# A three-block transformer step on one core: GpSimd takes three of eight low halves in five norms, and linear attention sums its two key sets on VectorE before the diagonal product

## The chip, the core and the metric

The kernel runs on one core of a Trainium2 chip. The metric is the device time of one execution in microseconds (us); lower is better. Engines: PE is TensorE, DVE is VectorE, ACT is ScalarE, POOL is GpSimd, SP is the queue that issues weight loads.

## What is computed

Input x is 512 tokens by 1024 features in float32. Two blocks of a first model and one of a second follow each other:

```python
for i in range(2):                        # first model
    h = modulate(rms_norm(x, g), shift, scale)
    y = nsa_mixer(h) if i == 0 else swa_sink_mixer(h)
    x = x + (1 + g1) * rms_norm(y, g)
    h = modulate(rms_norm(x, g), shift2, scale2)
    x = x + (1 + g2) * rms_norm(squared_relu_mlp(h), g)
h = rmsnorm(x, norm_mix)                  # second model
# linear attention, neighbourhood attention, cross attention on h, gated and summed,
# then x = x + (...) @ w_out and a convolutional FFN on rmsnorm(x, norm_ffn)
```

The linear attention has 8 heads of width 128 and is summed over both directions of time:

```python
f = lb + (1 - lb) * sigmoid(zf);  k = (1 - lb) * sigmoid(-zf)   # one zf for each direction
scores[t, s] = sum_k q[t, k] * k[s, k] * prod(f between s and t)
o = (scores @ v)_forward + (scores @ v)_backward
```

At t = s no decay stands between the two, so the diagonal of the scores is q·k for each direction, and the output needs the sum of both.

## The kernel before

All activations are kept transposed, features on the 128 partitions and 512 tokens along the free dimension, so a matrix of 1024 features is 8 chunks of 128x512. Every weight product keeps float32 precision with fp32r matmuls: a number is split into a rounded high half and a low half, and a product is high·high + high·low + low·high, three matmuls a chunk, 24 for a panel of 128 output features. The panels follow each other for the whole kernel; they alternate between two PSUM banks `PA` and two halves of the weight buffers. SP loads a panel into `RAW`; POOL makes its high half (L658) and then its low half (L665); both are 128x1024 reads and writes of SBUF. POOL starts on a panel when PE has finished the high products of the panel two before it (semaphore `w_hi_used`), and SP loads the next one when POOL has made the low half.

The list `RUNS` (L270 to L348) is the written order of panels. The queues of SP, POOL and PE all walk it with `walk` (L350): a run of equal panels becomes a hardware loop, and an entry that is a string makes POOL do other work at that place. "residual" is such an entry: POOL adds three of the eight residual chunks (`add_pooled`, L673) between the weight panels.

**A norm** (`norm`, L1818, `round_hi`, L1318, `first_pair`, L791). When the inverse root of the mean square is in PSUM, three engines work chunk by chunk: DVE multiplies chunk k into a PSUM bank `PO` (L1826), ACT writes its rounded high half to `H[0]` (L1327 with a shift, L1325 without), DVE writes the low half, full minus high, to `H[1]` (L1835 or L1833). PE follows in `first_pair` with two panels at once: per chunk two matmuls with the high half (L802), one with the low half of the weight (L804), then a wait for `h_lo` and two matmuls with the low half of the activation (L807). After chunk 7 there are eight more matmuls of the second panel (L813). There are seven such norms: memory tokens, the first norm of x, and five later ones, at about 522, 905, 1120, 1492 and 2319 us.

**Linear attention** (PE L1175 to L1214, ACT L1596, DVE L2228 to L2288). For each head PE goes through ten levels (`lv`), each followed by half of a weight panel of the next head (`panel_half`, 12 matmuls), which keeps PE in work while DVE and ACT prepare the next level. Level 0 is the diagonal: for each of four 128-token blocks a product of the forward keys `R[:, KF]` with q and one of the backward keys `R[:, KB]` with q, summed in PSUM (L1192, L1193). These are plain float32, and each appears in the trace as two matmuls. Levels 1 to 7 use keys that ACT copies to `HK` (L1602), and levels 8 and 9 the larger blocks. `prepare(h)` (L2228) stands on DVE between head h-1 and head h: the floor of the forget gates (L2233, whose semaphore `level_qk` releases level 0 on PE), a copy of it (L2235), and two products with q (L2236, L2237), the second of which releases ACT's keys of level 1.

Of the kernel before, what the change touches and what calls it, by code (L numbers as in the profile page):

```python
# [19 lines left out]
F32 = mybir.dt.float32  # L20
# [83 lines left out]
def build(nc, T, out):  # L104
# [237 lines left out]
    OUT0["mix"] = count_panels()  # L342
    run(8, DC, lambda i: panel(w_out2, 0, DC, i * P))
    for g in range(2):
        run(GC, DC, lambda i, g=g: panel(w_up2, 0, DC, (g * GC + i) * P),
            lambda i, g=g: panel(w_up2, 0, DC, (FFC + g * GC + i) * P))
        OUT0["ffn"] = count_panels()
        run(8, GC, lambda i, g=g: panel(w_dn2, g * GC, GC, i * P))  # L348

# [61 lines left out]
        return T["ada_w"][l, (m % DC) * P:(m % DC + 1) * P, g * ADA_N:(g + 1) * ADA_N]  # L411

    POOLED = [1, 3, 5]
    DVE_OWN = [k for k in range(DC) if k not in POOLED]
    RESIDUAL_ORDER = [1, 0, 3, 2, 5, 4, 6, 7]
    NORM_MIX, MEM_NORM, NORM_FFN, NORM_FINAL, GNORM, COND = 64, 72, 80, 88, 96, 97
# [232 lines left out]
    @block.gpsimd  # L649
    def _(pool):  # L650
        pool.memset(zeros[:], 0.0).then_inc(sem("zeros_set"), 1)
        pool.wait_ge(sem("zeros_set"), 1)

        def split_hi(e, p, s, kc):
            if not isinstance(p, int) or p >= 2:
                e.wait_ge(w_hi_used, p - 1)
            e.wait_ge(w_loaded[s], ((p - s) * 16) + 32 if not isinstance(p, int) else (p // 2 + 1) * 32)
            e.tensor_tensor(W[0][:, s, 0:kc], RAW[:, s, 0:kc], zeros[:, 0:1].rearrange("p (a b) -> p a b", b=1).broadcast_to([P, kc, P]),  # L658
                            ALU.add).then_inc(w_hi, 1)

        def split_lo(e, p, s, kc):
            e.wait_ge(w_hi, p + 1)
            if not isinstance(p, int) or p >= 2:
                e.wait_ge(panel_ready, p - 1)
            e.tensor_tensor(W[1][:, s, 0:kc], RAW[:, s, 0:kc], W[0][:, s, 0:kc].bitcast(F32), ALU.subtract).then_inc(w_split, 1)  # L665

        def split(e, p, s, kc, loads):
            split_hi(e, p, s, kc)
            split_lo(e, p, s, kc)

        c = Counts()

        def add_pooled():  # L673

            for k in POOLED:
                c["weighed"] += 1
                pool.wait_ge(sem("weighed_y"), c["weighed"])
                pool.tensor_tensor(X[:, k, :], X[:, k, :], Y[:, k, :], ALU.add).then_inc(sem("x_pooled"), 1)

        def scale_weights(which, fills):  # L680

            if which == "residual":
                add_pooled()
                return
            plan = PLANS[which]
            for i, (G, b) in enumerate(plan.units):
                grp, u = plan.groups[G], c["unit"] + i
                nk, v = grp["keys"][b], u % 8
                inverse = stat[3][:, v:v + 1]
                pool.wait_ge(sem("inverted"), u + 1)  # L690
                at = int(grp["sink"] is not None)
                w = plan.weights[i % len(plan.weights)][:, at:at + nk]
                if grp["all"]:
                    pool.tensor_tensor(blocks4(w), blocks4(w), each4(inverse4, grp), ALU.mult).then_inc(sem("scaled"), 1)
                elif grp["gate"] is None:
                    pool.tensor_scalar(w, w, inverse, None, ALU.mult).then_inc(sem("scaled"), 1)  # L696
# [12 lines left out]

    @block.tensor  # L710
    def _(pe):
# [79 lines left out]
        def first_pair(x, n):  # L791

            p, ready = c["panel"], c["normed"] - DC
            a, b = p % 2, 1 - p % 2
            if p >= 2:
                pe.wait_ge(panel_free, p)
            pe.wait_ge(w_split, p + 2)
            for k in range(DC):
                hi, lo, last = x[0][:, k, 0:n], x[1][:, k, 0:n], k == DC - 1
                pe.wait_ge(sem("h_hi"), ready + k + 1)  # L800
                for s in (a, b):
                    pe.matmul(PA[s][:, 0:n], W[0][:, s, k], hi, start=(k == 0), stop=False)  # L802
                if not last:
                    pe.matmul(PA[a][:, 0:n], W[1][:, a, k], hi, start=False, stop=False)  # L804
                pe.wait_ge(sem("h_lo"), ready + k + 1)
                for s in (a, b):
# [369 lines left out]
        for h in range(8):  # L1176
            R, q = HR[h % 2], HQ[h % 2]
            for lv in range(10):
                r = c["level"]
                if 1 <= lv <= 7:  # L1180
                    pe.wait_ge(sem("level_k"), 7 * h + lv)
                else:
                    pe.wait_ge(sem("level_qk"), r + 1)
                if r >= 2:
                    pe.wait_ge(sem("level_taken"), r - 1)
                if lv == 9:
# [2 lines left out]
                for b in range(NT):  # L1189
                    cols_b = slice(b * P, b * P + P)  # L1190
                    if lv == 0:
                        pe.matmul(bank[:, cols_b], R[:, KF, cols_b], q[:, cols_b], start=True, stop=False)  # L1192
                        mm = pe.matmul(bank[:, cols_b], R[:, KB, cols_b], q[:, cols_b], start=False, stop=True)  # L1193
                    elif lv <= 7:
                        mm = pe.matmul(bank[:, cols_b], HK[:, lv % 2, cols_b], two_sides(R, QB, QF, b * P, P, LEVELS[lv - 1]), start=True, stop=True)
                    elif lv == 8:
# [65 lines left out]
    def _(act):  # L1262
# [52 lines left out]
        def root(N=S, bank=PS[0]):  # L1315
            act.activation(roots[:, 0:N // P], bank[:, 0:N // P], ACT.Sqrt, bias=sl("eps"), scale=1.0 / D).then_inc(sem("rooted"), 1)

        def round_hi(dst, n, shift, N=S, at=0):  # L1318

            for k in range(n):  # L1320
                r = c["normed"]
# [2 lines left out]
                if shift is None:  # L1324
                    act.activation(hi, full, ACT.Copy).then_inc(sem("h_hi"), 1)  # L1325
                else:
                    act.activation(hi, full, ACT.Identity, bias=shift(k), scale=1.0).then_inc(sem("h_hi"), 1)  # L1327
                c["normed"] += 1

        def rotary_hi(p, turned):  # L1330
# [94 lines left out]
                    for m in range(DC * (3 + g) + 2, min(DC * (4 + g) + 2, 6 * DC)):  # L1425
                        mod_load(m)

        def apply(shift, dst=H, N=S):
            round_hi(dst, DC, shift, N)
            act.wait_ge(sem("h_lo"), c["normed"])  # L1430

        def norm(shift):
            squares(xs, DC, added=True)
            c["x_ready"] += len(DVE_OWN)
            c["x_pooled"] += len(POOLED)
            inverse_root()
            apply(shift)

        xs = lambda k: X[:, k, :]
        ys = lambda k: Y[:, k, :]  # L1440
# [61 lines left out]
        mem_value_copy(3)  # L1502
        phi_load(1)
        round_hi(H, DC - 3, lambda k: mod(0, 0)(k + 3), at=3)
        act.wait_ge(sem("h_lo"), c["normed"])
        act.wait_ge(sem("angle"), 1)
        act.activation(sinT[:], sinT[:], ACT.Sin)
        act.activation(cosT[:], cosT[:], ACT.Sin, bias=sl("half_pi"), scale=-1.0).then_inc(sem("tables"), 1)
# [186 lines left out]
                open_gate(k + 2)  # L1695
        act.dma_start(X[:], x_spill).then_inc(sem("x_back"), 16)
        panel_squares(xs, OUT0["mix"])
        apply(None)
        for g in range(2):
            for k in range(GC):  # L1700
                act.wait_ge(sem("conv_a"), g * GC + k + 1)
# [18 lines left out]
    def _(dve):  # L1720
# [94 lines left out]
            dve.tensor_tensor(tmp[3][:, 0:N].rearrange("p (b n) -> p b n", b=nb), ident.rearrange("p (b n) -> p b n", b=1).broadcast_to([P, nb, P]),  # L1815
                              roots[:, 4:4 + nb].rearrange("p (b n) -> p b n", n=1).broadcast_to([P, nb, P]), ALU.mult).then_inc(sem("diagonal"), 1)

        def norm(src, scale, shift, dst=H, N=S, inverse=PS[1]):  # L1818

            for i in range(DC + 1):  # L1820
                if i < DC:
                    r = c["normed"]
                    if r >= 2:
                        dve.wait_ge(sem("h_lo"), r - 1)
                        dve.wait_ge(sem("h_hi"), r - 1)
                    dve.scalar_tensor_tensor(PO[r % 2][:, 0:N], src(i), scale(i), inverse[:, 0:N], ALU.mult, ALU.mult).then_inc(sem("normed"), 1)  # L1826
                    c["normed"] += 1
                if i >= 1:
                    r, k = c["h_lo"], i - 1
                    full, hi, lo = PO[r % 2][:, 0:N], dst[0][:, k, 0:N].bitcast(F32), dst[1][:, k, 0:N]  # L1830
                    dve.wait_ge(sem("h_hi"), r + 1)
                    if shift is None:
# [1 line left out]
                    else:  # L1834
                        dve.scalar_tensor_tensor(lo, full, shift(k), hi, ALU.add, ALU.subtract).then_inc(sem("h_lo"), 1)  # L1835
                    c["h_lo"] += 1

        def inverse_here():

# [256 lines left out]
            taken(lambda bank: dve.tensor_copy(cols[:, r, 0:c_rows[r]], bank[:, 0:c_rows[r]]))  # L2096
        dve.wait_ge(sem("turned_taken"), c["turned"])
        dve.wait_ge(sem("inverse"), 1)
        norm(ym, col1(MEM_NORM), None, MH, 256)
        dve.wait_ge(sem("cond_sig"), 1)  # L2100
        link(dve.tensor_tensor(small[:, 0:8], cols[:, 1, COND:COND + 8], small[:, 8:16], ALU.mult))
        mod_step(0)
# [11 lines left out]

        dve.wait_ge(sem("inverse"), 2)
        dve.wait_ge(sem("turned_taken"), 20)
        norm(xs, coef(0, 0), mod(0, 0), inverse=PT[0])
        dve.wait_ge(sem("tables"), 1)

        def add_positions(side, k):  # L2120
# [107 lines left out]
        def prepare(h):  # L2228
# [2 lines left out]
            dve.wait_ge(panel_free, HG0 + 5 * h + 4)  # L2231
            dve.wait_ge(sem("turned_taken"), c["turned"])
            dve.tensor_scalar(HTP[:], HT[h % 2][:], 1e-12, None, ALU.max).then_inc(sem("level_qk"), 1)  # L2233
            dve.wait_ge(sem("level_qk"), 10 * h + 1)
            dve.tensor_copy(HT[h % 2][:], HTP[:]).then_inc(sem("hg_floor"), 1)  # L2235
            dve.tensor_tensor(R[:, QF, :], HTP[:, 0, :], q[:], ALU.mult)  # L2236
# [163 lines left out]
```

## Time and profile before

| | us |
|---|---|
| median of 3 runs | 2705.49 |
| the three runs | 2708.56, 2705.10, 2705.49 |
| the profiled execution | 2709.62 |
| its span, from first to last instruction | 2707.8 |
| PE busy | 2529.4 |
| POOL busy | 1772.6 |
| DVE busy | 1347.7 |
| ACT busy | 711.8 |

The profiled execution is one run, 4.1 us above the median, and 1.8 us of it lie outside the span. A busy share of PE near 100% does not mean full speed: the ends of matmuls are modelled, so the distance between starts is what counts, and a granted clock of 1.00 stands for 2.4 GHz and 0.50 for 1.2 GHz.

### The profile page before, as it was taken

Reading aid. Unit: us, or ns where it says so; the run is one execution under the profiler, and the core shown is the slowest. Engines: PE = TensorE matmul, PEld = TensorE weight load, DVE = VectorE, ACT = ScalarE, POOL = GpSimd, SP = SyncE. Lnnn points to the kernel's source line nnn. Section 1 sums busy time; section 2 is a strip of 40 time slices with the busy share of each in tenths; the row PEclk is TensorE's granted clock in tenths of the full one; section 3 lists DMA queues with packets and bytes.
Section 4 is the critical chain, followed back from the end, with each engine's and each line's share of the span. In section 5 each row is a group of like instructions: output and inputs, shape, how many; then the busy total and the mean of one; then the engine's idle time right before and its main releaser. Section 6 shows DMA issues by size and latency. Waiting matters only on the chain. (4 is left out here: it accounts for less than half of the span.)

```text
span 2707.8 us, 36598 instructions
## 1 busy us (share of the span) xinstructions
PE 2529.4 (93%) x11854; PEld 2049.4 (76%) x11854; DVE 1347.7 (50%) x2632; ACT 711.8 (26%) x1498; POOL 1772.6 (65%) x983
## 2 busy tenths in 40 slices
PE   7898889899999888899999999999999889999998
PEld 6686667688888667688886777777878776787877
DVE  6367887443442566412213567674128434752552
ACT  4204776211101245301112223232017232100001
POOL 5364445587777576577776545455769767787884
PEclk9898989999999889899999999999999999999999
DMA  8383000254653212233332221212323213233332
GB/s 292 117 240 97 1 1 24 89 184 150 205 186 89 59 40 75 69 101 93 99 95 85 86 63 58 60 57 69 100 85 77 74 55 117 85 96 91 93 105 74
DMA packets 420545, 259.73 MB, mean 96 GB/s; under 512 B 62844, under 2 KB 411513, under 8 KB 414017
## 3 DMA queue, kind: packets, MB, share of 16 engines
q1 hardware_dynamic: 390896, 195.28, 25.0%
q10 hardware_dynamic: 29521, 62.82, 7.1%
q8 instruction: 71, 1.16, 0.2%
q14 instruction: 57, 0.47, 0.1%
HBM read 253.86 MB, written 8.10 MB: 97 GB/s over the span
## 5 line engine op out<-in xcount | busy, mean ns | idle before, releaser
L658 POOL TENSOR_TENSOR W<-RAW,zeros 128x1024 fp32r<-128x1024 f32 (+2 forms) x355 | 678.1, 1910 | 687.7 <-PE PA L741 328.7
L665 POOL TENSOR_TENSOR W<-RAW,W 128x1024 fp32r<-128x1024 f32 (+2 forms) x355 | 850.5, 2396 | 31.7 <-PE PA L749 5.1
L738 PE MATMUL PA<-H,W 128*128 128x512 f32 x1272 | 500.8, 394 | 6.0 <-POOL W L658 2.1
L741 PE MATMUL PA<-H,W 128*128 128x512 f32 x1272 | 498.3, 392 | 0.0
L738 PE MATMUL PA<-A,W 128*128 128x512 f32 x944 | 374.8, 397 | 16.2 <-DVE A L1973 10.8
L741 PE MATMUL PA<-A,W 128*128 128x512 f32 x944 | 372.2, 394 | 0.0
L749 PE MATMUL PA<-H,W 128*128 128x512 f32 x1272 | 314.3, 389 | 0.0
L738 PEld LDWEIGHTS PA<-H,W 128*128 128x128 f32 x1272 | 240.2, 189 | 59.7 <-POOL W L658 6.5
L741 PEld LDWEIGHTS PA<-H,W 128*128 128x128 f32 x1272 | 240.2, 189 | 50.4 <-issue 0.5
L749 PEld LDWEIGHTS PA<-H,W 128*128 128x128 f32 x1272 | 238.7, 188 | 49.5
L749 PE MATMUL PA<-A,W 128*128 128x512 f32 x944 | 238.6, 395 | 0.0
L738 PEld LDWEIGHTS PA<-A,W 128*128 128x128 f32 x944 | 178.8, 189 | 59.4 <-issue 14.0
L749 PEld LDWEIGHTS PA<-A,W 128*128 128x128 f32 x944 | 180.4, 191 | 38.2
L741 PEld LDWEIGHTS PA<-A,W 128*128 128x128 f32 x944 | 178.9, 190 | 35.4
L1421 ACT ACTIVATE tmp<-PA 128x512 f32<-128x512 f32 x64 | 38.3, 598 | 520.2 <-PE PA L749 514.7
L696 POOL TENSOR_SCALAR pr<-pr,stat_inv 128x256 f32<-128x256 f32 (+2 forms) x112 | 136.6, 1229 | 49.0 <-DVE stat_inv L1932 48.4
L698 POOL TENSOR_SCALAR pr<-pr,stat_inv,gate 128x128 f32<-128x128 f32 (+3 forms) x128 | 88.2, 689 | 117.0 <-DVE stat_inv L1932 116.9
L2043 DVE SCALAR_TENSOR_TENSOR PA<-PA,tmp 128x512 f32<-128x512 f32 x64 | 44.8, 700 | 235.7 <-ACT tmp L1421 235.7
L1367 ACT ACTIVATE pr<-sc,stat_neg 128x128 f32<-128x128 f32 (+3 forms) x240 | 133.8, 557 | 103.4 <-DVE stat_neg L1920 101.2
L779 PE MATMUL PA<-H,W 128*128 128x512 f32 x320 | 133.4, 417 | 0.0
L780 PE MATMUL PA<-H,W 128*128 128x512 f32 x320 | 125.1, 391 | 0.0
L1702 ACT ACTIVATE tmp<-tmp 128x512 f32<-128x512 f32 x22 | 13.9, 633 | 276.5 <-DVEq L2348 276.5
(367 smaller groups left out, 3974.8 us busy)
## 6 DMA issues: line engine op xcount, KB each, us to landing
AD<-in_ada_w_dram ACTq DMA_DIRECT2D x40, 1024.0 KB, 5.1
RAW<-in_w_in_dram SPq DMA_DIRECT2D x160, 256.0 KB, 3.2
RAW<-in_mlp_w_up_dram SPq DMA_DIRECT2D x128, 256.0 KB, 3.1
RAW<-in_mlp_w_down_dram SPq DMA_DIRECT2D x128, 256.0 KB, 3.1
RAW<-in_w_up_dram SPq DMA_DIRECT2D x88, 256.0 KB, 3.1
RAW<-in_nsa_w_in_dram SPq DMA_DIRECT2D x40, 256.0 KB, 4.2
RAW<-in_w_down_dram SPq DMA_DIRECT2D x16, 384.0 KB, 3.4
RAW<-in_swa_w_in_dram SPq DMA_DIRECT2D x20, 256.0 KB, 3.3
```

The lines of the kernel that those rows point to most:

```text
L658: e.tensor_tensor(W[0][:, s, 0:kc], RAW[:, s, 0:kc], zeros[:, 0:1].rearrange("p (a b) -> p a b", b=1).broadcast_to([P, kc, P]), ALU.add).t ...
L665: e.tensor_tensor(W[1][:, s, 0:kc], RAW[:, s, 0:kc], W[0][:, s, 0:kc].bitcast(F32), ALU.subtract).then_inc(w_split, 1)
L696: pool.tensor_scalar(w, w, inverse, None, ALU.mult).then_inc(sem("scaled"), 1)
L698: pool.tensor_scalar(w, w, inverse, grp["gate"][b], ALU.mult, ALU.mult).then_inc(sem("scaled"), 1)
L738: pe.matmul(PA[s][:, 0:n], W[0][:, s, k], hi, start=(k == 0), stop=False)
L741: mm = pe.matmul(PA[s][:, 0:n], W[0][:, s, k], lo, start=False, stop=False)
L749: mm = pe.matmul(PA[s][:, 0:n], W[1][:, s, k], x[0][:, k, 0:n], start=False, stop=(k == kc - 1))
L779: pe.matmul(PA[s][:, :], W[0][:, s, k], H[0][:, k, :], start=(k == 0), stop=False)
L780: mm = pe.matmul(PA[s][:, :], W[0][:, s, k], H[1][:, k, :], start=False, stop=False)
L1367: act.activation(plan.weights[i % ring][:, 0:nk], sc[u % 2][:, 0:nk], ACT.Exp, bias=neg, scale=-1.0, accum_out=stat[2][:, v:v + 1]).then_i ...
L1421: act.activation(tmp[q][:], PA[s][:], ACT.Relu).then_inc(sem("mlp_relu"), 1)
L2043: dve.scalar_tensor_tensor(PA[s][:], PA[s][:], 0.0, tmp[q][:], ALU.max, ALU.mult).then_inc(sem("mlp_square"), 1)
```

## The change

Two edits that do not touch each other.

Norms: in the five later norms the low halves of chunks 1, 3 and 5 are made by POOL. Since POOL works from SBUF here, ACT writes for these chunks, beside the high half, a full copy to `tmp[4]` or `tmp[5]`; POOL subtracts, and PE waits for the new semaphore `h_low` in place of `h_lo`. The first run of the last norm's panels is split into 2 and 20 panels, so that POOL's three subtractions have a place between them.

Linear attention: DVE adds both key sets of a head into `HK[:, 0]`, right after the floor that releases level 0 on PE; PE waits for that sum and makes one product per block.

```diff
-        run(GC, DC, lambda i, g=g: panel(w_up2, 0, DC, (g * GC + i) * P),
-            lambda i, g=g: panel(w_up2, 0, DC, (FFC + g * GC + i) * P))
+        if g == 0:
+            run(1, DC, lambda i: panel(w_up2, 0, DC, 0), lambda i: panel(w_up2, 0, DC, FFC * P))
+            RUNS.append("norm")
+        a = 1 if g == 0 else 0
+        run(GC - a, DC, lambda i, g=g, a=a: panel(w_up2, 0, DC, (g * GC + i + a) * P),
+            lambda i, g=g, a=a: panel(w_up2, 0, DC, (FFC + g * GC + i + a) * P))
...
+    LOW_POOLED = [1, 3, 5]
...
+        def subtract_pooled():
+            for j, k in enumerate(LOW_POOLED):
+                n = c["h_full"]
+                pool.wait_ge(sem("h_full"), n + 1)
+                pool.tensor_tensor(H[1][:, k, :], tmp[4 + j % 2][:], H[0][:, k, :].bitcast(F32), ALU.subtract).then_inc(sem("h_low"), 1)
+                c["h_full"] += 1
...
             if which == "residual":
                 add_pooled()
+            if which in ("residual", "norm"):
+                subtract_pooled()
                 return
...
-                pe.wait_ge(sem("h_lo"), ready + k + 1)
+                name = "h_low" if k in pooled else "h_lo"
+                c[name] += 1
+                pe.wait_ge(sem(name), c[name])
...
+                if lv == 0:
+                    pe.wait_ge(sem("keys_added"), h + 1)
...
-                        pe.matmul(bank[:, cols_b], R[:, KF, cols_b], q[:, cols_b], start=True, stop=False)
-                        mm = pe.matmul(bank[:, cols_b], R[:, KB, cols_b], q[:, cols_b], start=False, stop=True)
+                        mm = pe.matmul(bank[:, cols_b], HK[:, 0, cols_b], q[:, cols_b], start=True, stop=True)
...
+                if k in pooled:
+                    j = pooled.index(k)
+                    if j >= 2:
+                        act.wait_ge(sem("h_low"), c["h_full"] - 1)
+                    whole = tmp[4 + j % 2][:]
+                    if shift is None:
+                        act.activation(whole, full, ACT.Copy).then_inc(sem("h_full"), 1)
+                    else:
+                        act.activation(whole, full, ACT.Identity, bias=shift(k), scale=1.0).then_inc(sem("h_full"), 1)
...
-                    if r >= 2:
-                        dve.wait_ge(sem("h_lo"), r - 1)
+                    if i >= 2:
                         dve.wait_ge(sem("h_hi"), r - 1)
+                        if i - 2 in pooled:
+                            dve.wait_ge(sem("h_full"), c["h_full"] + pooled.index(i - 2) + 1)
+                        else:
+                            dve.wait_ge(sem("h_lo"), c["h_lo"])
...
-                if i >= 1:
+                if i >= 1 and i - 1 not in pooled:
...
             dve.tensor_scalar(HTP[:], HT[h % 2][:], 1e-12, None, ALU.max).then_inc(sem("level_qk"), 1)
+            dve.tensor_tensor(HK[:, 0, :], R[:, KF, :], R[:, KB, :], ALU.add).then_inc(sem("keys_added"), 1)
             dve.wait_ge(sem("level_qk"), 10 * h + 1)
             dve.tensor_copy(HT[h % 2][:], HTP[:]).then_inc(sem("hg_floor"), 1)
             dve.tensor_tensor(R[:, QF, :], HTP[:, 0, :], q[:], ALU.mult)
```

## Rows read from the trace of the kernel before

**Rows 1.** The page, part 1: busy time of each engine, share, instructions

```profile
PE 2529.4 (93%) x11854; PEld 2049.4 (76%) x11854; DVE 1347.7 (50%) x2632; ACT 711.8 (26%) x1498; POOL 1772.6 (65%) x983
```

**Rows 2.** Timeline of the norm at 522 us: PE, then DVE, then ACT (start, us, engine)

```profile
523.73 1.19 PE L802 MATMUL PA<-H,W 128*128 128x512 f32 x2 [3.07 <-ACT H L1327]
531.65 0.72 PE L807 MATMUL PA<-H,W 128*128 128x512 f32 x2
534.80 1.98 PE L813 MATMUL PA<-H,W 128*128 128x512 f32 x8
...
522.11 1.42 DVE L1826 SCALAR_TENSOR_TENSOR PO<-X,coefA,PS 128x512 f32<-128x512 f32 x2 [5.78 <-ACT PS L1313]
...
522.90 1.35 ACT L1327 ACTIVATE H<-PO,modT 128x512 fp32r<-128x512 f32 x2 [0.88 <-DVE PO L1826]
```

**Rows 3.** Source L807: for whom its weight loads waited (us, times)

```profile
  DVE H L1835: 0.8, 2
```

**Rows 4.** Timeline of PE in the norm at 1120 us, second chunk

```profile
1123.81 1.05 PE L802 MATMUL PA<-H,W 128*128 128x512 f32 x2
```

**Rows 5.** Sources L678 and L1852: ns min/median/max of each form, first and last start

```profile
L678 POOL TENSOR_TENSOR X<-X,Y x12: 1265/1268/1273, 508.1 to 1482.4; 128x512 f32<-128x512 f32 x12
...
L1852 DVE SCALAR_TENSOR_TENSOR X<-PT,coefA,X x20: 751/751/752, 508.7 to 1485.7; 128x512 f32<-128x512 f32 x20
```

**Rows 6.** Timeline at the start of head 1: PE, DVE, POOL

```profile
1567.80 0.49 PE L1192 MATMUL PS<-sinT,Y 128*128 128x128 f32 x2
1569.61 0.48 PE L779 MATMUL PA<-H,W 128*128 128x512 f32 x1
...
1566.52 1.23 DVE L2233 TENSOR_SCALAR HTP<-hg_T 128x1024 f32<-128x1024 f32 x1
1577.46 0.69 DVE L2268 TENSOR_TENSOR Y<-Y,HTP 128x512 f32<-128x512 f32 x1 [6.06 <-PE PS L1195]
...
1567.09 1.89 POOL L658 TENSOR_TENSOR W<-RAW,zeros 128x1024 fp32r<-128x1024 f32 x1 [3.80 <-PE PA L780]
```

**Rows 7.** Timeline at the start of head 2: DVE and POOL

```profile
1611.65 1.23 DVE L2233 TENSOR_SCALAR HTP<-hg_T 128x1024 f32<-128x1024 f32 x1
...
1612.13 1.90 POOL L658 TENSOR_TENSOR W<-RAW,zeros 128x1024 fp32r<-128x1024 f32 x1 [3.61 <-PE PA L780]
```

**Rows 8.** Timeline at the start of head 0: PE, DVE, POOL

```profile
1527.03 0.79 PE L1192 MATMUL PS<-cosT,Y 128*128 128x128 f32 x2 [2.65 <-DVE HTP L2233]
1530.30 0.48 PE L779 MATMUL PA<-H,W 128*128 128x512 f32 x1
...
1525.75 1.22 DVE L2233 TENSOR_SCALAR HTP<-hg_T 128x1024 f32<-128x1024 f32 x1
...
1524.66 2.35 POOL L665 TENSOR_TENSOR W<-RAW,W 128x1024 fp32r<-128x1024 f32 x1
```

**Rows 9.** Timeline of the FFN: DVE and POOL

```profile
2336.87 1.51 DVE L2351 TENSOR_TENSOR tmp<-tmp 128x512 f32<-128x512 f32 x1
...
2335.94 1.89 POOL L658 TENSOR_TENSOR W<-RAW,zeros 128x1024 fp32r<-128x1024 f32 x1
```

**Rows 10.** Busy time by stretches: PE busy, ..., granted clock third from the end

```profile
2147.97:2151.97 4.00, 4.00 (x18) 3.31 (x19) 0.00 (x0) 0.00 (x0) 3.92 (x3) 1.00 0.44 131
2280.85:2284.85 4.00, 4.00 (x11) 3.13 (x12) 0.59 (x1) 0.00 (x0) 3.97 (x2) 0.57 0.03 8
1056.80:1060.80 4.00, 3.98 (x14) 2.07 (x14) 4.00 (x7) 3.98 (x7) 0.00 (x0) 1.00 0.92 281
1528.00:1890.00 362.00, 355.08 (x1789) 288.88 (x1788) 234.94 (x415) 95.03 (x139) 175.40 (x82) 1.00 0.21 60
```

**Rows 11.** Timeline of PE: the gaps that end where three of those stretches begin

```profile
1056.82 0.47 PE L738 MATMUL PA<-A,W 128*128 128x512 f32 x1 [2.38 <-DVE A L1973]
2147.97 0.50 PE L738 MATMUL PA<-H,W 128*128 128x512 f32 x1 [1.56 <-ACTq L1267]
2280.85 0.64 PE L738 MATMUL PA<-H,W 128*128 128x512 f32 x1 [2.07 <-POOL W L658]
```

More of the change, by code:

```diff
@@ L793, in first_pair @@
             p, ready = c["panel"], c["normed"] - DC
+            pooled = LOW_POOLED if p >= 16 else []
             a, b = p % 2, 1 - p % 2
@@ L1316, in root, with round_hi @@
             act.activation(roots[:, 0:N // P], bank[:, 0:N // P], ACT.Sqrt, bias=sl("eps"), scale=1.0 / D).then_inc(sem("rooted"), 1)
-        def round_hi(dst, n, shift, N=S, at=0):
+        def round_hi(dst, n, shift, N=S, at=0, pooled=()):
             for k in range(n):
@@ L1327, in round_hi @@
                     act.activation(hi, full, ACT.Identity, bias=shift(k), scale=1.0).then_inc(sem("h_hi"), 1)
+                if k in pooled:
[7 more added lines that the diff above has]
+                        act.activation(whole, full, ACT.Identity, bias=shift(k), scale=1.0).then_inc(sem("h_full"), 1)
+                    c["h_full"] += 1
+                else:
+                    c["h_lo"] += 1
                 c["normed"] += 1
@@ L1426, in mlp, with apply @@
                         mod_load(m)
-        def apply(shift, dst=H, N=S):
-            round_hi(dst, DC, shift, N)
-            act.wait_ge(sem("h_lo"), c["normed"])
+        def apply(shift, dst=H, N=S, pooled=()):
+            round_hi(dst, DC, shift, N, pooled=pooled)
+            act.wait_ge(sem("h_lo"), c["h_lo"])
+            act.wait_ge(sem("h_low"), c["h_full"])
         def norm(shift):
@@ L1436, in norm @@
             inverse_root()
-            apply(shift)
+            apply(shift, pooled=LOW_POOLED)
         xs = lambda k: X[:, k, :]
@@ L1504, in _ @@
         round_hi(H, DC - 3, lambda k: mod(0, 0)(k + 3), at=3)
-        act.wait_ge(sem("h_lo"), c["normed"])
+        act.wait_ge(sem("h_lo"), c["h_lo"])
         act.wait_ge(sem("angle"), 1)
@@ L1697, in _ @@
         panel_squares(xs, OUT0["mix"])
-        apply(None)
+        apply(None, pooled=LOW_POOLED)
         for g in range(2):
@@ L1816, in rstd, with norm @@
                               roots[:, 4:4 + nb].rearrange("p (b n) -> p b n", n=1).broadcast_to([P, nb, P]), ALU.mult).then_inc(sem("diagonal"), 1)
-        def norm(src, scale, shift, dst=H, N=S, inverse=PS[1]):
+        def norm(src, scale, shift, dst=H, N=S, inverse=PS[1], pooled=LOW_POOLED):
             for i in range(DC + 1):
@@ L1822, in norm @@
                     r = c["normed"]
-                    if r >= 2:
-                        dve.wait_ge(sem("h_lo"), r - 1)
+                    if i >= 2:
                         dve.wait_ge(sem("h_hi"), r - 1)
+                        if i - 2 in pooled:
+                            dve.wait_ge(sem("h_full"), c["h_full"] + pooled.index(i - 2) + 1)
+                        else:
+                            dve.wait_ge(sem("h_lo"), c["h_lo"])
                     dve.scalar_tensor_tensor(PO[r % 2][:, 0:N], src(i), scale(i), inverse[:, 0:N], ALU.mult, ALU.mult).then_inc(sem("normed"), 1)
                     c["normed"] += 1
-                if i >= 1:
-                    r, k = c["h_lo"], i - 1
+                if i >= 1 and i - 1 not in pooled:
+                    k, r = i - 1, c["normed"] - (1 if i == DC else 2)
                     full, hi, lo = PO[r % 2][:, 0:N], dst[0][:, k, 0:N].bitcast(F32), dst[1][:, k, 0:N]
@@ L1836, in norm @@
                     c["h_lo"] += 1
+            c["h_full"] += len(pooled)
+            if pooled:
+                dve.wait_ge(sem("h_full"), c["h_full"])
         def inverse_here():
@@ L2098, in _ @@
         dve.wait_ge(sem("inverse"), 1)
-        norm(ym, col1(MEM_NORM), None, MH, 256)
+        norm(ym, col1(MEM_NORM), None, MH, 256, pooled=[])
         dve.wait_ge(sem("cond_sig"), 1)
@@ L2116, in _ @@
         dve.wait_ge(sem("turned_taken"), 20)
-        norm(xs, coef(0, 0), mod(0, 0), inverse=PT[0])
+        norm(xs, coef(0, 0), mod(0, 0), inverse=PT[0], pooled=[])
         dve.wait_ge(sem("tables"), 1)
```

## Prediction

> **What bounds the kernel now.** I first read the page for the engine that is busy throughout: PE, 2529.4 us or 93% of the span [rows 1]. DVE and POOL have time left on average, so the question is where PE waits for them or is made to. Then I read the timelines of the two stages that the diff touches. In a norm PE starts 1.6 us after DVE and then follows chunk by chunk; in linear attention it stands still only at the head of each head, for the floor of the forget gates. There the granted clock is 1.00 over the whole stage [rows 10]. What counts is when PE starts and what it waits for; busy time on DVE counts only through that. Last I looked for what a new DVE instruction with both inputs in SBUF does beside POOL, since the change puts one in front of PE eight times, and for what PE's clock does after short gaps.
>
> **Norms, five times.** Per norm the change takes 3 low halves from DVE, adds 3 full copies on ACT and gives POOL 3 subtractions. DVE's pace with both operations is one chunk in about 1.45 us. PE's is 5 matmuls a chunk. Their starts are 0.227 us apart at clock 1.00 (eight of them span 1.98 us, the last one's modelled length being 0.39) and 0.43 at half clock [rows 2, 4]: 1.1 and 2.1 us a chunk. PE starts the norm after a gap and is at half clock for its first two or three chunks, so it falls behind DVE and needs almost the rest of the norm to catch up. All that the weight loads of the low products waited for DVE is 0.8 us, twice, over the whole kernel [rows 3]; both fall in the norm at 522 us. With the pitches around them, that norm would end 0.5 us earlier if DVE were never late. The other four gain nothing.
>
> Is POOL in time? In the norm at 522 us DVE's first two products end at 523.5, ACT's two high halves at 524.25 [rows 2]; the full copy costs another 0.69 (524.95), and POOL's subtraction 1.27, taken from its addition of the same size [rows 5]: 526.3. By the same walk the low half of chunk 3 is ready at 528.6 and that of chunk 5 at 530.9. PE reads the latter at 531.65 [rows 2], and, counting back two chunks of 1.13 us at a time, chunk 3 near 529.3 and chunk 1 near 527.0. POOL has nothing else to do there: its next weight panel waits until the last low product of the norm. So POOL's work is hidden, with margins of 0.6 us; without that cover each late low half would cost up to 0.5. ACT's 3 copies fit between its high halves, which now take half of its time. DVE's wait for the full copies ends where the next product would start anyway. The run of FFN panels that is split in two changes no load: the first two panels were split on POOL before that norm as well. Term: **-0.5 us**; bounds -3 (PE begins several norms at clock 1.00, and DVE's pace would then have cost it) and +1.5.
>
> **Linear attention, what PE saves.** Level 0 now runs from 1567.80 to 1569.61, 1.81 us for 16 matmuls, 0.113 each [rows 6]. Half of them go: 0.90 us a head. In head 0, where the clock is at half, it is 3.27 us for 16 [rows 8], so 1.64 go. The Trainium skill (TensorE: Matmul & The Clock Gate, "Wait — 56ns, not 53.3ns?") gives 55.6 ns from start to start for 128 columns at full clock. That would make the saving half as large, 0.45 a head, and the sum 3.2 us worse; the trace does not agree for these float32 products, and it decides.
>
> **What PE waits for instead.** The addition stands behind the floor on DVE and in front of the copy and both products with q. Alone it would cost what the nearest DVE operation does, some 0.55 to 0.7 us. But it is not alone. In head 1 the floor ends at 1567.75, while POOL makes a high half from 1567.09 to 1568.98 [rows 6]; in head 2 the floor ends at 1612.88 and POOL's high half at 1614.03 [rows 7]. The other five heads repeat these two patterns, four in all with 1.23 us left of the high half and three with 1.15. This is geometry, not chance: POOL is released by PE's own half panel, and DVE by PE's level 9 just before it.
>
> What a DVE operation with two SBUF inputs does then is seen in the FFN: L2351 starts at 2336.87, while POOL's high half runs until 2337.83, and ends at 2338.38 after 1.51 us instead of 0.69 [rows 9]. It does nothing until POOL's instruction ends, then needs 0.55. It gets its turn before POOL's next instruction, which follows 0.08 us later. The Trainium skill (SBUF — State Buffer, "Who interferes with whom") has it as a rule: a VectorE instruction with two SBUF inputs and a GpSimd instruction that reads SBUF lock each other out; the trace agrees, with that row.
>
> So the addition ends 1.23 + 0.55 = 1.78 or 1.15 + 0.55 = 1.70 us after the floor, 1.74 on average, and PE's level 0 starts that much later. Net per head: 1.74 - 0.90 = +0.84; for seven heads **+5.9 us**. In head 0 POOL ends at 1527.01, just as the floor does [rows 8]: the addition costs 0.6, the saving is 1.64, and about two later matmuls move into the half clock (0.4): **-0.6 us**.
>
> Nothing takes this back or adds to it later in the head. The copy, the products with q, the gate and the taking of level 0 all come 1.7 us later on DVE, but DVE then idles 6.06 us for PE's level 1 [rows 6]; ACT's keys of level 1 come 1.7 us later too, but PE first has half a panel and the values of the last head to work off, and DVE sees level 1 done only at 1577.46 [rows 6], 7.9 us after level 0 has begun. POOL's low half starts up to 0.5 us later and is wanted only two levels on.
>
> **The clock.** PE will stand still some 1.75 us before level 0 in seven heads, where the half panel runs into level 0 without a gap that the timeline shows today [rows 6]. After a gap of 1.56 us in dense work the clock stayed at 1.00, after one of 2.07 it was 0.57 over the next 4 us, after one of 2.38 it stayed at 1.00 [rows 10, 11]. So a gap of this size can cost the clock, and sometimes does. One such drop costs 4.0 x (1 - 0.57) = 1.7 us. The bounds are no head (0) and all seven (+11.9). I take three heads, nearer to the middle than to either end, as 1.75 lies between a gap that kept the clock and a shorter gap than 2.38 that lost it: **+5.1 us**.
>
> **Sum.** -0.5 - 0.6 + 5.9 + 5.1 = +9.9 us. For the profiled execution that is 2709.62 + 9.9 = 2719.5; it stands 4.1 above the median of the runs, so the median becomes 2705.49 + 9.9 = **2715.4 us**. A measurement of this kernel can tell 0.2%, 5.4 us, from no change: 2700.1 to 2710.9 is "same".
>
> **Rivals.**
> *The clock holds.* The gap never costs the clock; all else as above: +4.8, 2710.3, inside "same". For it: the 1.56 us gap, and full clock in the whole stage today. Against it: 2.07 us lost it, and level 0 behind the gap is thin work. Chance 0.22.
> *The addition is not held up.* It runs beside POOL's high half, or gets in before it. Then a head costs 0.6 - 0.9 = -0.3, seven -2.1, and with head 0 and the norms -3.2: 2702.3, not slower. The place is the start of heads 1 to 7; the point from which it decides is a delay of the addition behind POOL of 0.3 us: below it the head gains, above it it loses. For it: DVE passes POOL freely when one of its inputs is in PSUM, and a shift of the floor by 0.6 us to the front would be enough. Against it: the row in the FFN, with the same POOL instruction. Chance 0.12.
> *The norms give more.* Without the low halves DVE is never the pace, and in norms where PE begins at clock 1.00 up to 1.3 us each are won. With the addition not held up as well this reaches -7: 2698. The trace shows PE behind, not DVE. Chance 0.04.
> *Held by both halves.* DVE doesn't get in between POOL's two instructions (0.08 us apart) and waits for the low half too, 2.4 us more a head, +17 on top: 2727 with the clock held. Against it: it did get in at 2337.83. Chance 0.07.
> *The forecast*, with one to seven heads at half clock: 2712 to 2722, chance 0.55.
>
> The range for 8 in 10 takes in the forecast, the held clock and the free addition: 2702.0 to 2722.5. Faster by over 0.2%: 0.04. Same: 0.22 + 0.12 = 0.34. Slower: 0.55 + 0.07 = 0.62.
>
> **What would show it.** In the timeline of heads 1 to 7 the addition should be 1.7 to 1.8 us long and end 0.55 us after POOL's high half; PE's gap before level 0 should be near 1.75 us with DVE's `hg_K` as its releaser, and level 0 should last 0.9 us. An addition of 0.7 us beside a running POOL instruction would prove the main step wrong. The granted clock of the stage, 1.00 today, should fall below 1: each head that lost it takes about 0.5% off the stage's mean. In the norms PE's last eight matmuls should start at the same distance from DVE's first product as now, 0.5 us less at 522 us; a wait of PE for POOL's low half of over 0.5 us would prove the hidden part wrong. The prediction fails as a whole if the distance from one level 0 to the next shrinks.

## The result, and the profile after the change

| us | before | after |
|---|---|---|
| median of 6 runs | 2705.4 (2704.55 to 2709.32) | 2716.5 (2711.14 to 2718.91) |
| ratio, 95% interval | | 1.0037 (1.0027 to 1.0047) |
| profiled execution | 2709.62 | 2716.51 |
| its span | 2707.8 | 2714.4 |
| mean granted clock | 0.967 | 0.965 |

The kernel became slower by 0.37%. The same kernel measured once more, beside the kernel before and its own parts (`e6_after_again`), gave 1.0025 (1.0015 to 1.0036). The forecast was 2715.4 us. (Ratios here are made from all runs of both kernels, so they can differ a little from the quotient of the medians.) The two profiled executions are only 6.9 us apart, since the one of before stands 4.1 above the median of its first runs; so the views below explain some 6.6 us of span, and not 11.

The page of the kernel after, part 1:

```profile
PE 2523.2 (93%) x11790; PEld 2046.2 (75%) x11790; DVE 1348.1 (50%) x2625; ACT 719.3 (26%) x1513; POOL 1793.6 (66%) x998
```

PE is busy for 6.2 us less than in [rows 1] and the program is longer: the busy totals say nothing of this change, only the waits do. Now the timeline at the start of head 1 of the linear attention, as in [rows 6]. Line numbers have moved: the floor is L2271, the addition L2272, level 0 on PE L1212.

```profile
1566.77 1.23 DVE L2271 TENSOR_SCALAR HTP<-hg_T 128x1024 f32<-128x1024 f32 x1
...
1567.34 1.89 POOL L663 TENSOR_TENSOR W<-RAW,zeros 128x1024 fp32r<-128x1024 f32 x1 [3.80 <-PE PA L795]
1567.91 1.87 DVE L2272 TENSOR_TENSOR hg_K<-Y 128x512 f32<-128x512 f32 x1
...
1569.31 2.72 POOL L670 TENSOR_TENSOR W<-RAW,W 128x1024 fp32r<-128x1024 f32 x1
1569.70 1.21 DVE L2274 COPY hg_T<-HTP 128x1024 f32<-128x1024 f32 x1
...
1569.88 1.13 PE L1212 MATMUL PS<-sinT,hg_K 128*128 128x128 f32 x8 [1.80 <-issue]
1570.76 0.48 PE L794 MATMUL PA<-H,W 128*128 128x512 f32 x1
```

The floor ends at 1568.00. The addition ends at 1569.78, which is 1.78 us later and 0.55 after POOL's high half (1567.34 + 1.89 = 1569.23). PE follows at 1569.88, after 1.80 us of standing still. Level 0 then has 8 matmuls and takes 0.88 us, from 1569.88 to the next panel's first matmul at 1570.76, where [rows 6] had 16 in 1.81 by the same measure. The addition over all eight heads, from the source view of its line:

```profile
L2272 DVE TENSOR_TENSOR hg_K<-Y x8: 690/1826/1870, 1526.0 to 1844.1; 128x512 f32<-128x512 f32 x8
```

690 ns is head 0: there the addition starts at 1525.95, POOL's low half ends at 1526.10, and no other POOL instruction follows for 10 us. The seven others are held up. The starts of level 0 in heads 2 and 3 show the same twice over, with the two patterns of the forecast:

```profile
1615.86 1.13 PE L1212 MATMUL PS<-cosT,hg_K 128*128 128x128 f32 x8 [1.72 <-issue]
...
1661.93 1.13 PE L1212 MATMUL PS<-sinT,hg_K 128*128 128x128 f32 x8 [1.80 <-issue]
```

From one head to the next it takes 46.0 us, against 45.16 before. The waits of PE in this stage:

```profile
PE PS L1212 <- issue: 12.4, 7, 1.8
PE PS L1212 <- DVE hg_K L2272: 3.3, 1, 3.3
```

12.4 us in seven waits, 1.77 each, and the profile writes them down to "issue". Only in head 0 does it name `hg_K`. A blocked DVE instruction counts as busy from its issue on, so no idle time stands anywhere that would lead to POOL; the cause shows only where the rows of DVE and POOL are laid side by side.

The clock, in stretches of 8 us around three of the seven gaps and over the whole stage (columns as in [rows 10]):

```profile
1566.00:1574.00 8.00, 6.20 (x31) 4.83 (x30) 7.26 (x9) 1.48 (x2) 4.61 (x2) 1.00 0.18 52
1612.00:1620.00 8.00, 6.28 (x31) 4.89 (x30) 7.25 (x9) 1.48 (x2) 4.60 (x2) 1.00 0.19 55
1658.00:1666.00 8.00, 6.20 (x31) 4.88 (x30) 7.32 (x9) 1.48 (x2) 4.60 (x2) 1.00 0.16 48
...
1528.00:1895.00 367.00, 347.74 (x1720) 282.00 (x1720) 246.03 (x421) 94.72 (x139) 176.09 (x82) 0.99 0.20 58
```

The granted clock stays at 1.00 after the gap, here and in the four other heads. The 0.99 of the stage comes from head 0 alone, in the stretches at its start:

```profile
1526.80:1530.20 3.40, 3.40 (x12) 3.11 (x13) 2.86 (x4) 0.86 (x1) 0.00 (x0) 0.50 0.55 154
1530.20:1533.60 3.40, 3.40 (x11) 2.65 (x11) 0.00 (x0) 0.00 (x0) 0.00 (x0) 0.60 0.00 0
1533.60:1537.00 3.40, 3.40 (x19) 2.99 (x18) 2.02 (x4) 0.70 (x1) 0.16 (x1) 1.00 0.00 0
```

In the trace of before the second of these stretches is at 1.00 already.

### The profile page after: what moved, and what is told of

Same layout as the page of the kernel before. It is cut to its first block and busy times, and to the rows that moved or that the text cites. A ratio compares the mean times of both kernels' runs of the same rounds, so it can differ in the third digit from the quotient of the medians.

```text
span 2714.4 us, 36469 instructions
## 1 busy us (share of the span) xinstructions
PE 2523.2 (93%) x11790; PEld 2046.2 (75%) x11790; DVE 1348.1 (50%) x2625; ACT 719.3 (26%) x1513; POOL 1793.6 (66%) x998
```

## The experiments

Ten kernels ran, in three groups on three chips, each timed against the kernel before beside it. They start from the kernel after; `...` marks lines left out of an edit. "Keys only" means: the list `LOW_POOLED` is empty, so that the norms are those of before, and linear attention is as after.

**The two halves by themselves.** `e1_norms_only` takes the addition and its wait out and puts the two products back; `e2_keys_only` empties the list, and with it goes ACT's wait for POOL's low halves.

```diff
-    LOW_POOLED = [1, 3, 5]
+    LOW_POOLED = []
...
-            act.wait_ge(sem("h_low"), c["h_full"])
```

> The norms' half of the change alone, against the kernel before. Main theory (PE is behind DVE in four of the five norms, POOL's low halves come in time): -0.5 us, between -3 and +1.5, and from DVE's first product to PE's last eight matmuls the same times as before within 0.3 us wherever the clock falls alike. Rival (DVE's low halves were the pace): -1 to -1.3 us a norm, -5 to -6 in all. Rival (POOL is late, PE waits for it): more than +0.5 us a norm.

Measured: 2709.2 us against 2708.81, ratio 0.9997 (0.9988 to 1.0006). The norms' half makes no difference that can be told, and the rival of -5 to -6 us is excluded. Its trace missed one point: the norm at 908 us, with PE at full clock throughout, took 11.7 us, where such norms take 12.6 to 13.1 without this half; 0.3 had been allowed.

> The linear attention's half alone, no low half on POOL. Main theory (the sum of the keys stands behind POOL's high half): the addition lasts 1.78 to 1.87 us in heads 1 to 7 and 0.69 in head 0, each head from 1 on is 0.84 us longer, the stage +6 to +7.5 us, and the whole kernel +6 to +11 us. Rival (the loss of the whole change comes from the norms or from a clock that falls there): within 3 us of the kernel before.

Measured: 2714.47 against 2708.81, ratio 1.0024 (1.0014 to 1.0034), 46.0 us a head, clock 1.00 over the stage. By the medians that is +5.7 us, just below the +6 expected, and by the ratio +6.5. All of the slowdown that can be told is in linear attention, and the two ratios multiplied, 1.0021, agree with the 1.0025 of the second measurement of the whole change.

**Who starts first.** `e3_add_first` is the whole change with the two DVE instructions in the other order. PE's level 0 waits for `keys_added` alone.

```diff
-                if 1 <= lv <= 7:
+                if lv == 0:
+                    pe.wait_ge(sem("keys_added"), h + 1)
+                elif lv <= 7:
                     pe.wait_ge(sem("level_k"), 7 * h + lv)
...
-                if lv == 0:
-                    pe.wait_ge(sem("keys_added"), h + 1)
...
+            dve.tensor_tensor(HK[:, 0, :], R[:, KF, :], R[:, KB, :], ALU.add).then_inc(sem("keys_added"), 1)
             dve.tensor_scalar(HTP[:], HT[h % 2][:], 1e-12, None, ALU.max).then_inc(sem("level_qk"), 1)
-            dve.tensor_tensor(HK[:, 0, :], R[:, KF, :], R[:, KB, :], ALU.add).then_inc(sem("keys_added"), 1)
```

> The whole change with one difference: the sum of the keys is issued before the floor of the forget gates, and PE's level 0 waits for that sum alone. Main theory (the lock with POOL is decided by who starts first): the addition starts 0.57 us before POOL's high half, lasts 0.69, POOL's instruction begins or runs up to 0.1 us later, PE has no gap before level 0, and each head is 0.9 to 1.0 us shorter than before, 1.9 shorter than after: about 2696 us, -9 against the kernel before. Rival (any DVE operation with two SBUF inputs in that place is slow, or DVE's later chain then holds PE up at level 1): a head no shorter than before, 2703 us or more.

Measured: 2700.11 against 2708.81, ratio 0.9966 (0.9952 to 0.9979). Timeline at the start of head 1 in this kernel, where L2271 is now the addition:

```profile
1564.00 0.69 DVE L2271 TENSOR_TENSOR hg_K<-Y 128x512 f32<-128x512 f32 x1
...
1564.56 1.89 POOL L663 TENSOR_TENSOR W<-RAW,zeros 128x1024 fp32r<-128x1024 f32 x1 [3.80 <-PE PA L795]
1564.61 1.22 DVE L2272 TENSOR_SCALAR HTP<-hg_T 128x1024 f32<-128x1024 f32 x1
1565.14 1.05 PE L1212 MATMUL PS<-sinT,hg_K 128*128 128x128 f32 x8
...
1566.54 2.40 POOL L670 TENSOR_TENSOR W<-RAW,W 128x1024 fp32r<-128x1024 f32 x1
```

The same addition, started 0.56 us ahead of POOL's instruction, takes 0.69 us. The floor, which has one SBUF input, runs beside POOL unharmed. PE's level 0 has no gap in front of it, and a head takes 44.00 us, 1.16 less than before. The saved products are 0.89 of that (see `e7_wait_two_products` below). The other 0.27 may come from level 0 no longer waiting for the floor, which in the trace of before held up its weight load for 0.40 us; that was not tried by itself. In head 0 the addition now meets POOL's low half, and takes 1.79 us.

**What it is held by.** `e4_psum_operand` is keys only, with the addition in its place behind the floor, but with its second input in PSUM. It adds the floored gates to the forward keys, so the diagonal of the scores is not the reference's; everything else is.

```diff
-            dve.tensor_tensor(HK[:, 0, :], R[:, KF, :], R[:, KB, :], ALU.add).then_inc(sem("keys_added"), 1)
+            dve.wait_ge(sem("level_qk"), 10 * h + 1)
+            dve.tensor_tensor(HK[:, 0, :], R[:, KF, :], HTP[:, 1, :], ALU.add).then_inc(sem("keys_added"), 1)
```

> The linear attention's half alone, but the addition reads its second input from PSUM, the floored forget gates, in place of the backward keys (so the diagonal of the scores isn't the reference's). Its place, size and readers stay. Main theory (two SBUF inputs beside POOL): it lasts 0.69 us in all heads although POOL runs beside it, PE waits 0.65 us before level 0, and a head is 0.25 us shorter than before: -2 to -3 us on the kernel. Rival (the addition is slow for another cause in that place, its position behind the floor or the keys that ACT wrote): 1.8 us long as after, +6 or more.

Measured: 2707.22 against 2708.81, ratio 0.9998 (0.9989 to 1.0007). The timeline of this kernel at head 1:

```profile
1565.47 1.89 POOL L663 TENSOR_TENSOR W<-RAW,zeros 128x1024 fp32r<-128x1024 f32 x1 [3.80 <-PE PA L795]
1566.17 0.69 DVE L2272 TENSOR_TENSOR hg_K<-Y,HTP 128x512 f32<-128x512 f32 x1
...
1566.96 1.13 PE L1212 MATMUL PS<-sinT,hg_K 128*128 128x128 f32 x8 [0.75 <-issue]
```

The addition starts and ends inside POOL's high half and takes 0.69 us. Same place, same size, same POOL instruction: what holds it up is that both inputs are in SBUF. PE's gap is 0.75 us, 0.65 were expected, and the head 45.0 us, 0.16 shorter than before in place of 0.25. The -2 to -3 us on the kernel can't be told from nothing: the medians differ by 1.6 us.

**The addition, the wait and the saving taken apart.** `e5_add_no_waiter` is keys only with the addition on DVE, but PE neither waits for it nor uses it, and makes both products. `e7_wait_two_products` keeps the wait (`if lv == 0: pe.wait_ge(sem("keys_added"), h + 1)`), and still makes both products; against keys only it lacks the saving alone. The edit that both share:

```diff
-                        mm = pe.matmul(bank[:, cols_b], HK[:, 0, cols_b], q[:, cols_b], start=True, stop=True)
+                        pe.matmul(bank[:, cols_b], R[:, KF, cols_b], q[:, cols_b], start=True, stop=False)
+                        mm = pe.matmul(bank[:, cols_b], R[:, KB, cols_b], q[:, cols_b], start=False, stop=True)
```

> The addition stands on DVE as in the change, but PE doesn't wait for it and makes both products as before (low halves all on DVE). Main theory (the addition costs only through PE's wait; DVE's lateness of 1.8 us is covered by its idle time before level 1): the addition still lasts 1.8 us in heads 1 to 7, from one level 0 to the next 45.15 us as before, the kernel within 2 us of the one before. Rival (the later copy, products and gate hold a level or a panel up): over 0.3 us more a head, +2 us or more.

> The addition and PE's wait for it as in the change, but level 0 keeps both products (low halves all on DVE), so the saving is taken away and the wait is left. Main theory: 1.7 to 1.8 us more a head than before, 46.9 us from one level 0 to the next, +12 to +14 us on the kernel; against the keys alone +0.9 us a head, the value of eight matmuls. Rival (the removed matmuls were hidden and save nothing): 46.0 us a head as with the keys alone.

The first: 2709.68 against 2708.42, ratio 1.0004 (0.9995 to 1.0013). Its source view of the addition shows it held up as ever:

```profile
L2270 DVE TENSOR_TENSOR hg_K<-Y x8: 684/1826/1870, 1528.7 to 1840.6; 128x512 f32<-128x512 f32 x8
```

Yet a head takes 45.17 us, as before. So 1.8 us more on DVE, with the copy, both products with q and ACT's keys of level 1 behind them, cost nothing; the time is lost only where PE waits. The second: 2722.45, ratio 1.0049 (1.0035 to 1.0063), 46.91 us a head. PE waits in it 12.4 us, seven times, as in the kernel after. Less the 46.02 of keys only, the saved products are worth 0.89 us a head; less the 45.17, the wait costs 1.74.

**A second addition.** `e8_second_add` is keys only with one more addition of the same inputs, ahead of the real one, into `HK[:, 1]`, where nobody reads it.

```diff
+            dve.tensor_tensor(HK[:, 1, :], R[:, KF, :], R[:, KB, :], ALU.add)
             dve.tensor_tensor(HK[:, 0, :], R[:, KF, :], R[:, KB, :], ALU.add).then_inc(sem("keys_added"), 1)
```

> The keys alone, with a second addition of the same size ahead of the first, written where nothing reads it. Main theory of the lock (who starts first holds it for its whole instruction): the first addition waits for POOL's high half; POOL's low half, ready since then, takes the next turn, and the second addition waits 2.4 us more for it, so PE's gap grows from 1.8 to about 4.9 us and a head to 49 us, and in such a gap the granted clock falls to 0.5 in most heads, 1.7 us each: +25 to +40 us on the kernel. Rival (DVE keeps its turn over both additions): the second lasts 0.69, the gap is 2.4 us, a head 46.6 us, +10 to +15.

Measured: 2752.51, ratio 1.0161 (1.0147 to 1.0175): 44 us above before, more than was expected. Timeline at head 1:

```profile
1567.46 1.89 POOL L663 TENSOR_TENSOR W<-RAW,zeros 128x1024 fp32r<-128x1024 f32 x1 [3.80 <-PE PA L795]
1568.03 1.87 DVE L2271 TENSOR_TENSOR hg_K<-Y 128x512 f32<-128x512 f32 x1
...
1569.43 2.67 POOL L670 TENSOR_TENSOR W<-RAW,W 128x1024 fp32r<-128x1024 f32 x1
1569.82 2.82 DVE L2272 TENSOR_TENSOR hg_K<-Y 128x512 f32<-128x512 f32 x1
...
1572.75 2.05 PE L1212 MATMUL PS<-sinT,hg_K 128*128 128x128 f32 x8 [4.55 <-issue]
```

The first addition gets the turn between POOL's two halves. The second waits until the low half ends at 1572.10, and ends 0.54 us after that. PE's gap is 4.55 us, and after it level 0 takes 2.05 us in place of 1.13: after this gap the clock is at half, in all seven heads, and over the stage the page's clock is 0.93:

```profile
1528.00:1920.00 392.00, 353.46 (x1674) 286.76 (x1674) 264.27 (x426) 93.70 (x137) 169.00 (x78) 0.93 0.18 52
```

A head takes 51.1 us, 5.1 more than with one addition: 2.8 is the longer gap, and the rest, 2.3, is put down to the clock by subtraction. Here is the loss that the forecast had feared from the shorter gap.

**The whole change again.**

> The whole change as it stands, once more, beside the kernel before on the same chip as these parts. If its two halves only add up, it stands at the keys alone plus the norms alone, +5 to +7 us; the first measurement gave +11.1. In the trace, heads 1 to 7 are 46.0 us as before, and the norms end 11.7 us after DVE's first product where PE was at full clock throughout, 12.3 to 12.5 with 3 us at half clock, 13.5 to 13.6 with 6 us.

Measured: 2715.86 (2709.59 to 2718.97) against 2708.42, ratio 1.0025 (1.0015 to 1.0036), 46.0 us a head. It agrees with the first measurement's 1.0037 where the intervals overlap, from 1.0027 to 1.0036. +5 to +7 us was expected from the two halves; the ratio is +6.8 and the medians +7.4. The norms with about 3 us of half clock took 12.1 to 12.5 us, 12.3 to 12.5 were expected.

**The better order, with and without the norms' half.** `e10_add_first_again` is `e3_add_first` unchanged; `e9_add_first_keys` is the same with `LOW_POOLED` empty.

> The addition ahead of the floor as in the run e3_add_first, but without the norms' half of the change. Theory (the whole gain of e3 over before is that of linear attention, the norms are worth some 1.5 us at most and not to be seen): the distance from one level 0 to the next is 43.99 us as in e3, seven heads 7 x 1.16 = 8.1 us below before, and the ratio to before is 0.997 to 0.9975, within 2 us of the run beside it with the norms' half. Rival (the norms' half needs the freer stage or pays elsewhere in e3): this kernel is 3 us or more slower than e3, or 2 us or more faster.

> The kernel of e3_add_first unchanged, on the chip of the run beside it. Expected: ratio to before 0.9966 within its earlier interval (0.9952 to 0.9979), and 43.99 us from one level 0 to the next in heads 1 to 7. A rival that the earlier 0.9966 was luck of five runs would give 0.998 or more.

Measured beside each other and 2707.48 of before: with the norms' half 2699.28, ratio 0.9978 (0.9968 to 0.9988); without it 2702.45, ratio 0.9983 (0.9974 to 0.9992). Both take 44.0 us a head, as expected. The ratio of the first agrees with the earlier 0.9966, at that interval's edge, and does not exclude the rival's 0.998. The second missed its expected 0.997 to 0.9975. Seven heads at 1.16 us are 8.1 us, or 0.30%; what the runs show is 0.17 to 0.34%. Its profiled execution was the fastest of its eleven runs, so what the others lose is not in any trace. The norms' half is worth 3.2 us between the medians and 0.05% between the ratios. By the medians that is beyond the 2 us of the expectation and meets the rival's "3 us or more"; by the ratios, with these intervals, it is not told from nothing. So the rival is not excluded.

## Why the prediction was right, and where it was not

**What bounds, right.** Where PE waits decides: `e5_add_no_waiter` and `e7_wait_two_products` differ in nothing but the wait, and by 1.74 us a head.

**The saving, right.** 0.90 us a head forecast, 0.89 measured. At full clock the eight recorded matmuls are 0.11 us apart, as [rows 6] had said and against the 0.056 of the Trainium skill (TensorE: Matmul & The Clock Gate, "Wait — 56ns, not 53.3ns?"), by which it would have been 0.45. The page gives its figure by the number of columns alone, and these products are plain float32, with two recorded matmuls each.

**The wait, right.** 1.74 us forecast on the average of the two patterns, 1.80 and 1.72 measured. The Trainium skill (SBUF — State Buffer, "Who interferes with whom") has it that the two engines lock each other out when VectorE reads two SBUF inputs and GpSimd reads SBUF; the runs agree: 1.87 us with two, 0.69 with one of them in PSUM, 0.69 when DVE came first. +5.9 was forecast for seven heads, and the distances give 7 x 0.87 = +6.1. The rival that the addition is not held up is excluded, and so is the one with both halves, which takes a second addition to bring about. That the forecast named a shift of the floor by 0.6 us as enough was nearly the remedy: in `e3_add_first` the addition is ahead by 0.56.

**No later cost, right.** `e5_add_no_waiter` shows it: 45.17 us a head, with the later DVE work in it.

**The clock, wrong.** The step "I take three heads ... +5.1 us" failed: none of seven lost it. Gaps of 1.72 and 1.80 us kept the clock in every one of the heads of the kernel after, and in its repetition; gaps of 4.5 us, in `e8_second_add`, lost it in every head. [Rows 11] had one loss at 2.07 us and one hold at 2.38, and I put these into one order by length, though they contradict each other. Other traces show that length alone does not decide. At the very place of the 2.07, where PE waits for POOL's weights some 40 us ahead of the last norm, the gap and the clock of the 4 us behind it were, in the kernel after and in `e9_add_first_keys`:

```profile
2287.00 0.63 PE L753 MATMUL PA<-H,W 128*128 128x512 f32 x1 [1.93 <-POOL W L663]
2287.00:2291.00 4.00, 4.00 (x11) 3.14 (x12) 0.51 (x1) 0.00 (x0) 3.97 (x2) 0.57 0.04 11
...
2270.44 0.50 PE L753 MATMUL PA<-H,W 128*128 128x512 f32 x1 [2.16 <-POOL W L663]
2270.44:2274.44 4.00, 4.00 (x17) 3.30 (x18) 0.70 (x1) 0.20 (x1) 3.97 (x2) 1.00 0.04 13
```

Over the twelve profiled executions the clock was lost there five times, after 1.84 to 2.07 us, and kept seven times, after 1.60 to 2.16. In linear attention itself the forecast passed over the gap of [rows 8]: PE stands still before level 0 of head 0 for 2.65 us in the kernel before and 3.33 in the kernel after, out of a clock of 1.00, and half clock follows in all twelve (in `e10_add_first_again` only from within level 0). So in this stage 1.80 us kept the clock each time and 2.65 lost it each time. Between these two nothing was tried, and what decides at one length stays open.

**Head 0, wrong.** -0.6 forecast; about +1.2 measured. PE starts level 0 there 0.7 us later, counted from the last matmuls of the norm at 1492 us, as forecast (0.6). But the half clock lasts from 1526.8 to about 1533, where it had ended at 1530.2. In those two stretches of 3.40 us the clock is 0.50 and 0.60, against 0.51 and 1.00: 1.4 us more are lost, and with the later start and 0.9 for the work saved this is 0.7 + 1.4 - 0.9 = +1.2. The step counted the saved products at half clock (1.64) and took it that the clock would rise at the same time, which it did not. It differs between executions: the level 0 of heads 0 and 1 are 43.1 us apart here and in `e6_after_again`, but 41.8 in `e2_keys_only`, and one and the same kernel gave 41.1 as `e3_add_first` and 39.9 as `e10_add_first_again`. So the 1.4 us of clock are not shown to be the change's doing.

**The norms, too small in the traces, not told by any timing.** -0.5 forecast. From DVE's first product to PE's last eight matmuls, the five norms took in us (in brackets how long they ran at half clock, worked out from the clock between PE's first product and those eight, good to some 0.3 us):

| norm at | before | after |
|---|---|---|
| 522 | 12.69 (2.9) | 12.45 (3.5) |
| 905 | 13.70 (6.0) | 11.70 (0) |
| 1120 | 13.54 (5.7) | 13.58 (6.0) |
| 1492 | 13.35 (5.7) | 13.52 (6.0) |
| 2320 | 12.33 (3.4) | 12.31 (3.4) |

The sum is -2.0, but only in the norm at 905, where PE was at full clock this time. How long PE runs at half clock differs between executions of one kernel. Sorted by it, over the twelve profiled executions (five norms each): with 5 to 6 us of half clock a norm takes 13.1 to 13.7 us without this half of the change and 13.1 to 13.6 with it; with about 3 us, 12.3 to 13.2 without (nine of twelve at 13.1 or 13.2) and 12.1 to 12.5 with it; with none, 12.6 to 13.1 without and 11.4 to 11.7 with it. So the forecast's reason is right, that PE lags DVE when it starts at half clock, and its reading that this is so in four of five norms was one execution's. DVE's low halves are the pace where the clock is up. Summed over the five norms, the seven executions without this half took 65.6 to 66.0 us and the five with it 61.3 to 65.9, which is 2.4 less on average; `e1_norms_only`, the highest of the five, is no faster than these seven. No timing here tells the gain from nothing. POOL's part is hidden nearly as forecast. Its subtraction and the waits on it, from the source views of L683 and of the weight loads and products of L825:

```profile
L683 POOL TENSOR_TENSOR H<-tmp,H x15: 1281/1284/1298, 526.0 to 2332.6; 128x512 fp32r<-128x512 f32 x15
...
  POOL H L683: 2.4, 6
```

2.4 us in six cases, 2.0 of it on weight loads. In the norm at 522 the first subtraction starts 2.79 us after DVE's first product (525.99 less 523.20), where the walk of the forecast had 2.84 (524.95 less 522.11).

**The sum.** By the traces: heads 1 to 7 +6.1, head 0 +1.2, norms -2.0, together +5.3 of the 6.6 us between the spans. The 1.3 left lie in stretches that the change does not touch, which differ by -0.8 to +1.2 us between the two executions: 1.1 of it is there before the first norm that was changed, where DVE starts at 523.20 in place of 522.11 ([rows 2]). Over all twelve executions that start lies between 521.3 and 525.4, so this is no cost of the change. The forecast's +9.9 lies between the +11.1 and +7.4 of the two pairs of medians, but partly by luck: a clock term of +5.1 that did not occur stood in for head 0 (+1.8 over its forecast) and for the 1.3 from elsewhere, less the 1.5 that the norms gave beyond theirs, and the first comparison came out high. The case "the clock holds", at +4.8, was the truer account of the mechanism, and it had been given 0.22.

**The profile's name, wrong.** `hg_K` was to stand as the releaser of level 0; in seven heads it is "issue".

## What to carry to other kernels

Before a two-input VectorE operation from SBUF is put in front of TensorE, lay it beside GpSimd's instructions on the timeline: its cost is what is left of GpSimd's instruction plus its own time, not its own time. Here the kernel was 0.24 to 0.37% slower with the addition behind the floor and 0.17 to 0.34% faster with it in front, since it only has to start before GpSimd does. And lengthening the busy time of an engine that has slack is free (1.8 us in seven heads here) for as long as the bounding engine waits for something else.

## What the runs showed of the hardware that was not expected

- A blocked DVE instruction gets its turn in the 0.08 us between two POOL instructions and makes the next one pay: POOL's low half took 2.72 us behind the addition, and 2.40 where the addition was out of the way. One turn is one instruction: the second addition waited for POOL's whole next one (2.82 us).
- Before level 0 of heads 1 to 7, gaps of 1.72 to 1.80 us on PE kept the clock in all 28 cases (four traces), and gaps of 4.46 to 4.55 us lost it in all seven (one trace); but at the one place ahead of the last norm a gap of 1.84 us lost it once and one of 2.16 kept it once. The loss after the long gaps made the second addition cost 5.1 us a head where its delay alone was 2.8.
- The clock that PE is granted at the start of a norm differs between executions of one kernel, by up to 6 us of half clock for a norm. The runs of most kernels here spread over 5 to 12 us, and this may be a part of it; that was not tried.
